# Gate matmuls of a recurrent block rebuilt from 128-row to 64-row operands, with half-height tanh, in an eight-core decoder kernel

## The reference, cut to what matters

```
xh = x.reshape(Bsz, T, N_RNN_HEADS, RNN_HEAD_DIM)
r = sigmoid(einsum('bthi,hij->bthj', xh, w_r).reshape(...) + b_r)
i = sigmoid(einsum('bthi,hij->bthj', xh, w_i).reshape(...) + b_i)
log_a = -RG_C * r * softplus(-lam)
a = exp(log_a);  u = sqrt(-expm1(2.0 * log_a)) * (i * x)
h = a_t * h + u_t          # scan over time
```

## Time and profile before

| | us |
|---|---|
| three runs | 1536.99, 1537.02, 1541.75 (median 1537.02) |
| the profiled execution | 1537.04 |
| its span, slowest core (2) | 1535.5 (the other cores 1530.7 to 1534.2) |
| TensorE busy | 1520.1, 99% of the span |
| VectorE busy | 798.4, 52% |
| ScalarE busy | 764.4, 50% |

### The profile page before, as it was taken

How to read it: one execution, slowest core, us unless ns; L and a number is a source line. 1 busy time by engine, 2 the same in 40 slices (tenths; PEclk the granted TensorE clock), 3 DMA queues, 4 the chain that set the end, 5 groups by cost and what they waited for, 6 DMA issues and landing times.

```text
span 1535.5 us, 27118 instructions; the slowest of 8 cores (1530.7 to 1535.5 us)
## 1 busy us (share of the span) xinstructions
PE 1520.1 (99%) x8846; PEld 856.5 (56%) x8846; DVE 798.4 (52%) x1563; ACT 764.4 (50%) x1294; POOL 231.4 (15%) x441
## 2 busy tenths in 40 slices
PE   8999999999999999999999999999999999999998
PEld 5555555555555555555555555555555555555556
DVE  6422027886786665922236642056656895753124
ACT  4321146788854675612335431156767698552134
POOL 2011011101101111011101212121212121211120
PEclk9999999999999999999999999999999999999999
DMA  9699939876886686998976886565776455665463
GB/s 205 153 185 224 234 120 212 180 176 151 181 219 164 180 190 193 208 190 199 197 187 189 244 274 167 182 200 161 205 229 204 150 192 176 214 190 187 152 219 118
DMA packets 79898, 291.74 MB, mean 190 GB/s; under 512 B 8912, under 2 KB 9040, under 8 KB 79760
## 3 DMA queue, kind: packets, MB, share of 16 engines
q0 software_dynamic: 62480, 224.39, 59.5%
q1 hardware_dynamic: 17280, 65.61, 11.1%
HBM read 291.05 MB, written 61.30 MB: 229 GB/s over the span
## 4 chain that ended last, share of the span: by engine, by line
PE 95%; DMA 4%; issue 0%; POOL 0%; ACT 0%; DVEq 0%; DVE 0%; POOLq 0%; ACTq 0%; SPq 0%
PE P L726 95%; DMA wring<-wall 2%; DMA xs<-xin 1%; DMA wsc<-wring 1%; DMA wring<-wsc 0%; POOL wring L789 0%; ACT fp L740 0%; POOL xs L812 0%; DVEq L1286 0%; ACT qp L740 0%; DVE hy L744 0%; ACT big L740 0%; ACT hy L740 0%; POOLq L1280 0%; DVE big L744 0%
## 5 line engine op out<-in xcount | busy, mean ns | idle before, releaser
L726 PE MATMUL P<-hy,wring 128*128 128x416 bf16 (+2 forms) x6080 | 1089.7, 338 | 2.4 <-DMA wring<-wall 1.6
L726 PEld LDWEIGHTS P<-hy,wring 128*128 128x128 bf16 x6080 | 593.7, 98 | 474.1 <-issue 7.6
L740 ACT ACTIVATE fp<-P 128x416 f32<-128x416 f32 (+2 forms) x521 | 263.4, 514 | 600.9 <-PE P L726 579.1
L726 PE MATMUL P<-big,wring 128*128 128x416 bf16 (+3 forms) x2510 | 439.5, 331 | 1.0 <-DMA wring<-wsc 1.0
L744 DVE TENSOR_TENSOR big<-P,fp 128x416 bf16<-128x416 f32 (+1 forms) x255 | 148.6, 587 | 379.2 <-PE P L726 360.0
L726 PEld LDWEIGHTS P<-big,wring 128*128 128x128 bf16 x2510 | 241.5, 98 | 180.5 <-issue 1.8
L789 POOL DMA_DIRECT2D wring<-wsc x300 | 158.4, 528 | 802.0 <-PE P L726 770.4
L744 DVE TENSOR_TENSOR fp<-fp 128x416 f32<-128x416 f32 (+2 forms) x205 | 116.2, 570 | 176.6 <-ACT fp L740 170.2
L740 ACT ACT_TABLE_LOAD x119 | 152.7, 1283 | 35.6 <-PE P L726 31.7
L789 POOL DMA_DIRECT2D wring<-wall x127 | 67.4, 535 | 461.6 <-PE P L726 404.2
L758 DVE SCALAR_TENSOR_TENSOR fp<-P,par_sb,fp 128x416 f32<-128x416 f32 (+1 forms) x120 | 76.5, 644 | 5.8
(11 more groups left out here) (50 smaller groups left out, 435.9 us busy)
## 6 DMA issues: line engine op xcount, KB each, us to landing
wring<-wsc POOLq DMA_DIRECT2D x300, 512.0 KB, 4.9
wring<-wall POOLq DMA_DIRECT2D x109, 512.0 KB, 10.2
wsc<-wring SPq DMA_DIRECT2D x100, 512.0 KB, 8.6
yout<-big SPq DMA_DIRECT2D x6, 832.0 KB, 6.1
wring<-wall POOLq DMA_DIRECT2D x18, 256.0 KB, 5.6
xs<-xin SPq DMA_DIRECT2D x4, 832.0 KB, 7.9
xs<-xin POOLq DMA_DIRECT2D x7, 416.0 KB, 13.6
xs<-xin POOLq DMA_DIRECT2D x2, 832.0 KB, 35.4
```

Of the source, the lines that this page charges most:

```text
L726: ins = e.matmul(o, ev(lhs_list[k]), ev(rhs_list[k]), start=(start and k == 0), stop=(stop and k == nk - 1))
L740: return S.op("act", lambda e: e.activation(out=ev(out), in_=ev(in_), func=func, **kw), reads, writes, dur, tbl=TBL.get(func), prio=prio)
```

## The change

The weights of both gates of one head are put side by side: `wrgs` now holds for each j one 128x128 block whose upper 64 rows are head 2j with the columns [r | i], and whose lower 64 rows are head 2j+1 with the columns [i | r]. So its size is halved, from 2048 to 1024 columns. `mm_heads` issues one matmul on rows 0 to 63 into one bank and one on rows 64 to 127 into another: again 80 in all, each of 64 rows, 128 columns and 416 tokens. In the built program the first is on the array tile of 64x128 at row 0, the second on the one at row 64; all other matmuls are 128x128. Gate r of a channel block then lies in the first bank's partitions 0 to 63 and the second's 64 to 127, gate i in the other two halves, exchanged. Four tanh over 64 partitions (`half_act`) put them in order, instead of two over 128; 80 activations more. Both matmuls are recorded as one operation, so the two tanh waits are for the pair.

The planner's tables are new throughout (two lines of them stand in the diff below), and a rule in the planner keeps two banks of one operation apart. The number of DMA transfers is the same.

```diff
 LAGS = [
-     165.1, -32.66, -42.72, -334.5, 128.28, 739.43, -59.92, -39.12, -7.44, -481.51, -22.87, -485.17, -132.25, -28.82, 255.75, 171.25,
+     -37.29, 124.76, -35.74, -398.01, 121.46, 781.46, 93.18, -328.38, 210.78, -136.24, 7.03, -273.43, -322.84, 112.01, 346.55, -139.83,
...
-        def slot_for(v, eng):
+        def slot_for(v, eng, skip=None):
             best = None
             for i, old in enumerate(v.pool.slots):
+                if i == skip:
+                    continue
...
+                        first = {}
                         for v in o.allocs:
-                            r = slot_for(v, e)
+                            r = slot_for(v, e, first.get(v.pool.name))
...
-    wrg_d = nc.dram_tensor("wrg", [128, 2048], F32, kind="ExternalInput").ap()
+    wrg_d = nc.dram_tensor("wrg", [128, 1024], F32, kind="ExternalInput").ap()
...
+        def mm_heads(pa, pb, n, j, x):
+            def fn(e):
+                w = wrgs[:, j * 128:(j + 1) * 128]
+                e.matmul(ev(pa[0:n]), w[0:64], ev(x[0:n])[0:64], start=True, stop=True)
+                return e.matmul(ev(pb[0:n]), w[64:128], ev(x[0:n])[64:128], start=True, stop=True)
+            return S.op("pe", fn, [x, "wrgs"], [pa, pb], n / 2400.0 + 0.10)
+
+        def half_act(out, po, in_, pi, n, bias, writes):
+            return S.op("act", lambda e: e.activation(out=ev(out[0:n])[po], in_=ev(in_[0:n])[pi], func=AF.Tanh,
+                                                      scale=0.5, bias=bias[pi]),
+                        [in_] + DP, writes, 0.258 + n * 0.000833, tbl=TBL[AF.Tanh])
...
             pzr, pzi = newp(), newp()
-            mm_group(pzr[0:n], n, [wrgs[:, j * 128:(j + 1) * 128]], [cbh[0:n]], [cbh, "wrgs"], [pzr])
-            mm_group(pzi[0:n], n, [wrgs[:, 1024 + j * 128:1024 + (j + 1) * 128]], [cbh[0:n]], [cbh, "wrgs"], [pzi])
+            mm_heads(pzr, pzi, n, j, cbh)
             r, a, b = newf(), newf(), newf()
-            act(r[0:n], pzr[0:n], AF.Tanh, n, [pzr] + DP, [r], scale=0.5, bias=dcol(0, j), psum=True)
-            act(b[0:n], pzi[0:n], AF.Tanh, n, [pzi] + DP, [b, turn], scale=0.5, bias=dcol(1, j), psum=True)
+            half_act(r, slice(0, 64), pzr, slice(0, 64), n, dcol(0, j), [r])
+            half_act(r, slice(64, 128), pzi, slice(64, 128), n, dcol(0, j), [r])
+            half_act(b, slice(64, 128), pzi, slice(0, 64), n, dcol(1, j), [b])
+            half_act(b, slice(0, 64), pzr, slice(64, 128), n, dcol(1, j), [b, turn])
...
-                  [("wl", 0, RG_AFTER)], ["wrgs"], 1 << 20, cast=True)
+                  [("wl", 0, RG_AFTER)], ["wrgs"], 1 << 19, cast=True)
```

More of the change, by code:

```diff
@@ L255, in _nominal @@
     return list(zip(STARTS[g], ENDS[g], LOADS[g]))
-CLASSES = {"first": (0, -254.74),
-           "load": (0, 96.85),
-           "out": (0, -39.18),
-           "post": (1, -47.52),
-           "pre": (1, -99.13),
-           "weights": (2, -19.73),
-           "work": (0, 54.75)}
+CLASSES = {"first": (0, -129.89),
+           "load": (0, 51.42),
+           "out": (0, -72.52),
+           "post": (1, -18.03),
+           "pre": (1, -92.6),
+           "weights": (2, 84.76),
+           "work": (0, -12.49)}
 def _fm(w, cols):
@@ L519, in finalize @@
                                 break
+                            first[v.pool.name] = r[1]
                             if r[0] > st:
@@ L654, in build_program @@
         wring = sb("wring", [128, NW, WSLOT], BF16)
-        wrgs = sb("wrgs", [128, 2048], BF16)
+        wrgs = sb("wrgs", [128, 1024], BF16)
         par = sb("par_sb", [128, NPV * 8], F32)
@@ L1351 @@
     wall = _build_wall(w)
-    wrg = np.zeros((128, 2, KC, 128), np.float32)
-    for gi, name in enumerate(("w_rg_r", "w_rg_i")):
-        wr = f[name][0].astype(np.float32)
-        for c in range(KC):
-            wrg[0:64, gi, c, 0:64] = wr[2 * c]
-            wrg[64:128, gi, c, 64:128] = wr[2 * c + 1]
-    wrg = wrg.reshape(128, 2048)
+    wrg = np.zeros((128, KC, 128), np.float32)
+    wr, wi = f["w_rg_r"][0].astype(np.float32), f["w_rg_i"][0].astype(np.float32)
+    for c in range(KC):
+        wrg[0:64, c, 0:64], wrg[0:64, c, 64:128] = wr[2 * c], wi[2 * c]
+        wrg[64:128, c, 0:64], wrg[64:128, c, 64:128] = wi[2 * c + 1], wr[2 * c + 1]
+    wrg = wrg.reshape(128, 1024)
+    bi = np.asarray(f["b_rg_i"][0]).reshape(KC, 2, 64)[:, ::-1].reshape(-1)
     vecs = [f["g_ffn1_pre"][0], f["g_ffn1_post"][0], f["g_mix_pre"][0], f["g_mix_post"][0],
@@ L1362 @@
             f["conv_b_w"][0, 0], f["conv_b_w"][0, 1], f["conv_b_w"][0, 2], f["conv_b_w"][0, 3],
-            f["conv_b_b"][0], f["b_rg_r"][0], f["b_rg_i"][0], f["rg_lambda"][0]]
+            f["conv_b_b"][0], f["b_rg_r"][0], bi, f["rg_lambda"][0]]
     par = np.stack([np.asarray(v, np.float32).reshape(KC, 128).T for v in vecs], axis=1)
```

## The result

The changed kernel takes 1552.05 us, median of four runs, against 1537.23 for six of the kernel before; two more of its runs were disturbed on one die (1638.62 and 1783.18; with them the median of all six is 1554.68) and, like all such runs of either kernel, are left out of every comparison. The ratio is 1.0093, interval 1.0069 to 1.0117: 14 us slower. The profiled execution took 1554.22 us with a span of 1552.7 on core 6; the other cores' spans are 1544.8 to 1548.5. Core 6 has 3 to 4 us more of waits for weights than core 3, so core 3 is the better one to compare.

The account below looks back on a forecast made before the run. TensorE's stream of matmuls was taken to bound the kernel, time moving one to one with it. 1537.0 less 3.1 for the gate matmuls, all other terms 0, gave 1533.9 us, 0.2% faster; range 1529.0 to 1543.5.

Parts of the forecast that it names:

- The gate matmuls: 40 gate pairs on TensorE: second half starts 98 ns behind the first, 274 ns a pair, saving 3.1 us.
- my first rival: Gate pairs: the halves run fully side by side, saving 7.0 us, time 1530.0; chance 0.21.
- the third rival: Gate pairs: each change of form empties the array, 163 ns each, 13.0 us, time 1543.0 to 1546.9; chance 0.17.
- my own case: Gate pairs: second half starts one weight load, 98 ns, behind the first; time 1533.9; chance 0.43.
- The tanh: Gate activations on ScalarE: 80 more cost 40 to 49 us there, hidden under TensorE, so 0 on the path.
- the fourth rival: Added tanh time on ScalarE, or a bank, makes TensorE wait: 5 to 10 us, time 1539 to 1544; chance 0.08.
- The hold on banks: A pair's banks free up about 1.0 us later, after four tanh; counted at nothing.
- Weights and transfers: Gate weight load halves but was issued long before first use, other transfers unchanged; saves nothing on the path.
- the new order: New due times move the few mid-kernel waits of TensorE: 0 plus or minus 2.6 us.
- the ScalarE rival: Added tanh time on ScalarE, or a bank, makes TensorE wait: 5 to 10 us against the 3.1; chance 0.08.

Follow-up runs that it names:

- the old order: Kernel before in its own order with whole tanh, only the two gate matmuls on 64 rows each: ratio 1.0008, 1.2 us above the kernel before.
- a doubled pair: Changed kernel with each pair of 64-row gate matmuls issued twice in a row: ratio 1.0101, 15.5 us above the kernel before.
- the old work in the new order: Changed kernel's order with 128-row matmuls, one whole and one single-column tanh per tile: ratio 1.0006, 0.9 us above the kernel before.

## Why the prediction was wrong

**The gate matmuls, -3.1 us: the term was mis-sized and of the wrong sign.** I let the second half start one weight load behind the first. It does not: both start together, as my first rival had it, and the Trainium skill ("TensorE: Matmul & The Clock Gate", part 3) is borne out on that, with starts within 0.01 us. But the change of form costs about 0.10 us on each side, as the third rival said in kind; at 0.20 a pair it eats the 0.176 that the overlap gives, and 40 x 0.03 is about 1 us lost (1.2 measured in the old order). The point from which that rival decides was put at 39 ns a change for my own case; for full overlap it is 88. The Trainium skill's drain on a mode change ("TensorEngine Tiling (Array Packing)", tiling modes) fits the rows, 0.10 us at each border; my bound for it, the whole 163 ns of overlap, was too much. The 0.10 is near a load's 92 to 98 ns, and the loads are not ahead at the borders but are inside a doubled pair. That the border costs just one exposed load is therefore likely, but no run shows it against a drain of the same length.

**The tanh, 0 us: the step that failed.** The prediction put ScalarE's added time at nothing, as hidden under TensorE; it measured 11.5 us. "I take all" of a whole one's time was right (601 ns), and 40 to 49 us more of busy time was near (51.6 for the tanh). Wrong was to take 0.50 from start to start for the new ones, from rows in which whole tanh follow each other. Three of the four halves read or write from partition 64 on, and beside an activation that starts at another partition they neither begin before its end nor let it begin before theirs: 0.13 us at each such neighbour. In the stretch shown this is 1.76 us over sixteen activations. With four whole tanh, equally many and as long, the loss is 2.8 us instead of 14; so the cover I counted on was there for 80 more activations, and gone for what they really take. This is the fourth rival's mechanism, in its place (mixer stretches), at 0.08 the one that I held least likely; its price was 5 to 10 us for a quarter of the pairs, the measured one 11.5 us. It named the added length of the tanh as the reason, and that alone, with four whole ones, would not have done it.

**The hold on banks, 0 us.** It cannot be parted from the tanh: TensorE waits for their reading of the banks (1.01 us at 417.85) and for `qp`, the gates' input, which queues behind them on ScalarE.

**Weights and transfers, 0; the new order, 0 plus or minus 2.6.** Both held: 0.9 us (-0.6 to 2.6) with the old work in the new order. The sum of the measured parts is 1.2 (matmuls) + 0.9 (order) + 11.5 (lost overlap: the changed kernel less the one with four whole tanh) = 13.6, against 14.3 (10.6 to 18.0) measured. Each part has an interval of 1 us or more to either side, so that they agree this well is in part luck.

So the range failed on ScalarE's term alone: 11.5 us on top of the 1537.0 of before is 1548.5, beyond its end of 1543.5. The gain of 3.1 us, which the ScalarE rival still took off its price, fell away as well.

No version tried here is faster than the kernel before. Planning the new form with the true costs was not tried on the chip; with 0.38 against 0.352 for a pair and 80 more activations I see nothing that it could win. Several pairs in a row would have: by the rows four pairs together cost 0.2 + 4 x 0.176 = 0.9 us against 1.41, but that is an estimate and was not run.

## What to carry to other kernels

Before an operation is split by partitions, ask what its neighbours lose: the duration of one stays, but the distance from start to start may not, and a distance must be read from rows of the same kind. Where splitting cannot be avoided, parts that start at the same partition could be put in a row; the one place that has this kept the overlap, but no run tried it. Matmuls on half the rows do run side by side, yet each meeting of the two forms costs about 0.1 us, so they pay only in groups. And where a planner places work from costs, a wrong overlap can hurt more than the operations themselves: with 80 more activations whose cost the planner knew the kernel was 2.8 us slower in all, and 0.13 us of unknown cost at their neighbours made it 14.

## What the runs showed of the hardware that was not expected

- An activation that starts at another partition than its predecessor (0 against 64, in what it reads or in what it writes) starts 0.02 to 0.03 us after its end; with the same start partition, 0 or 64, it starts about 0.10 before the end (at 64: one place, 40 cases in five runs). Seen with 64 partitions and 416 columns beside 64 or 128 partitions. Height alone changes neither this nor the duration (0.59 to 0.61 us).
- A semaphore wait of ScalarE on its own previous activation costs 0.07 us more: two halves in a row take 1.30 us with it and 1.23 without.
- Two 64-row matmuls on different rows start within 0.01 us of each other. Going from 128-row matmuls to a pair and back costs 0.10 us each time; from pair to pair nothing (0.18 us from start to start).
